# Probabilities times values in two halves of 256 queries, and the outputs' copies one step later, for the Fox and neighbourhood heads of a two-block fp32 transformer kernel

## The reference

```python
def one_block(i):
    ...
    sc = jnp.einsum('bhqd,bhkd->bhqk', qb, k).astype(jnp.float32) * scale
    sc = sc + (cb[..., :, None] - c[..., None, :])
    sc = jnp.where(pos[None, :] <= tq[:, None], sc, NEG_INF)
    p = jax.nn.softmax(sc, axis=-1)
    return jnp.einsum('bhqk,bhkd->bhqd', p.astype(v.dtype), v)
```

## Time and profile before

| | |
|---|---|
| median of 3 runs | 1406.56 us (1406.37 to 1409.49) |
| the profiled execution's own time | 1405.87 us |
| its span in the profile | 1403.9 us |
| PE busy | 1339.9 us (95%) |
| DVE busy | 690.7 us (49%) |
| ACT busy | 614.5 us (44%) |
| POOL busy | 663.2 us (47%) |
| DMA, mean | 91 GB/s |
| steps of the fox attention in which values are multiplied | from about 88 us to 169 us |
| the same of the na attention | from about 779 us to 881 us |

### The profile page before, as it was taken

How to read it: one execution, slowest core, us unless ns; L and a number is a source line. 1 busy time by engine, 2 the same in 40 slices (tenths; PEclk the granted TensorE clock), 3 DMA queues, 4 the chain that set the end, 5 groups by cost and what they waited for, 6 DMA issues and landing times.

```text
span 1403.9 us, 19167 instructions
## 1 busy us (share of the span) xinstructions
PE 1339.9 (95%) x6444; PEld 1110.3 (79%) x6444; DVE 690.7 (49%) x1247; ACT 614.5 (44%) x964; POOL 663.2 (47%) x884
## 2 busy tenths in 40 slices
PE   7899999789999999999999879999999999999997
PEld 5877887578888888888778668877778888888887
DVE  6477656672222222121588878757445555552111
ACT  5445555564434442343434454435345444442223
POOL 5432152255645555565464213555645545454550
PEclk9999999999999999999999999999999999999999
DMA  5322231222433332333472212323324333333331
GB/s 161 87 76 68 69 106 46 76 76 77 118 95 99 91 103 83 101 94 101 92 151 77 67 52 65 103 90 90 90 75 120 90 102 92 99 92 98 98 94 61
DMA packets 220326, 127.22 MB, mean 91 GB/s; under 512 B 8635, under 2 KB 215880, under 8 KB 220136
## 3 DMA queue, kind: packets, MB, share of 16 engines
q1 hardware_dynamic: 219751, 126.20, 32.1%
q10 hardware_dynamic: 513, 0.21, 0.1%
HBM read 117.56 MB, written 2.47 MB: 85 GB/s over the span
## 4 chain that ended last, share of the span: by engine, by line
PE 83%; DVE 8%; issue 4%; ACT 2%; DMA 1%; ACTq 0%; SPq 0%; POOL 0%; DVEq 0%; POOLq 0%
PE PS L749 27%; PE PS L751 26%; PE PS L750 26%; DVE PTL L1895 1%; PE PS L938 1%; DMA RAW<-in_w_out 1%; DVE NM L1860 1%; PE PS L914 0%; DVE SS L1619 0%; PE PS L915 0%; ACT PR L1318 0%; DVE KB L1709 0%; DMA ROWV<-in_diff_norm_g 0%; DVE PR L1854 0%; DVE XL L1623 0%
## 5 line engine op out<-in xcount | busy, mean ns | idle before, releaser
L721 POOL TENSOR_TENSOR WL<-RAW,WH 128x256 fp32r<-128x256 f32 x864 | 657.6, 792 | 709.2 <-ACT WH L1172 709.2
L749 PE MATMUL PS<-XH,WH 128*128 128x512 f32 x1072 | 423.4, 395 | 2.7 <-DVE X L1967 1.9
L1172 ACT ACTIVATE WH<-RAW 128x1024 fp32r<-128x1024 f32 (+1 forms) x220 | 229.1, 1043 | 443.1 <-PE PS L751 378.8
L751 PE MATMUL PS<-XH,WL 128*128 128x512 f32 x1072 | 418.3, 390 | 0.0
L750 PE MATMUL PS<-XL,WH 128*128 128x512 f32 x1072 | 418.1, 390 | 0.0
L749 PEld LDWEIGHTS PS<-XH,WH 128*128 128x128 f32 x1072 | 201.9, 188 | 44.2 <-DVE X L1967 2.6
L751 PEld LDWEIGHTS PS<-XH,WL 128*128 128x128 f32 x1072 | 201.5, 188 | 42.6
L750 PEld LDWEIGHTS PS<-XL,WH 128*128 128x128 f32 x1072 | 201.7, 188 | 39.6 <-issue 0.7
L749 PE MATMUL PS<-HH,WH 128*128 128x512 f32 (+1 forms) x374 | 141.0, 377 | 0.0
L751 PE MATMUL PS<-HH,WL 128*128 128x512 f32 (+1 forms) x374 | 140.8, 377 | 0.0
L750 PE MATMUL PS<-HL,WH 128*128 128x512 f32 (+1 forms) x374 | 140.8, 377 | 0.0
(11 more groups left out here) (326 smaller groups left out, 1851.5 us busy)
## 6 DMA issues: line engine op xcount, KB each, us to landing
RAW<-in_w_up SPq DMA_DIRECT2D x66, 512.0 KB, 3.8
RAW<-in_w_in SPq DMA_DIRECT2D x60, 512.0 KB, 3.9
RAW<-in_w_down SPq DMA_DIRECT2D x32, 512.0 KB, 3.7
RAW<-in_w_gate SPq DMA_DIRECT2D x22, 512.0 KB, 3.8
RAW<-in_w_out SPq DMA_DIRECT2D x16, 512.0 KB, 3.7
RAW<-in_w_down SPq DMA_DIRECT2D x16, 384.0 KB, 3.3
QB<-QA SPq DMA_DIRECT2D x24, 128.0 KB
KA<-KA SPq DMA_DIRECT2D x24, 128.0 KB
```

Source lines behind the costliest of these rows:

```text
L721: ins = pool.tensor_tensor(WL[:, s, cs], RAW[:, s % 2, cs], WH[:, s, cs].bitcast(F32), ALU.subtract)
L749: pe.matmul(out, ah, bh, start=start, stop=False)
L751: return pe.matmul(out, al, bh, start=False, stop=stop)
L1172: act.activation(WH[:, s, 0:width], RAW[:, s % 2, 0:width], ACT.Copy).then_inc(w_hi, 1)
```

## The change

For fox and na the product with the values is made in two halves. The first half, queries 0 to 255, stands in step 4 hd + 5, the second, queries 256 to 511, in step 4 hd + 7. Each half multiplies every key block that one of its two query blocks sees, at width 256: for fox 2 and 4 key blocks (6 and 12 matmuls), for na 3 and 3 (9 and 9 matmuls). A block of PTH and PTL that a half reads and no query block writes must be zero, hence two more `memset` of DVE before each of the two attentions. A new semaphore `pv_first` counts first halves: PTH's query blocks 0 and 1 of the next head wait for it, blocks 2 and 3 for `pv_ready` as before. ACT's copy of a head's result (MH, NAH) and DVE's subtraction (ML, NAL) move from step 4 hd + 7 to step 4 hd + 8. The diff heads do the same as before.

```diff
+            def pv_half(hd, half):
+                g = o0 + hd
+                pe.wait_ge(ptl_done, t0 + 4 * hd + 2 * half + 2)
+                if half == 0 and g >= 2:
+                    pe.wait_ge(o_free, g - 1)
+                vc = slice((hd // 2) * P, (hd // 2) * P + P)
+                q = slice(256 * half, 256 * half + 256)
+                kcs = [kc for kc in range(4) if any(keys_of(kind, qb)[0] <= kc < keys_of(kind, qb)[1]
+                                                    for qb in (2 * half, 2 * half + 1))]
+                for kc in kcs:
+                    ins = mm3(PS[:, OB + g % 2, q], mem["VH"][:, kc, vc], mem["VL"][:, kc, vc],
+                              mem["PTH"][:, kc, q], mem["PTL"][:, kc, q], kc == kcs[0], kc == kcs[-1])
+                ins.then_inc(pv_ready if half else pv_first, 1)
...
-                if i - 4 in ready_after and ready_after[i - 4] % 4 == 3:
-                    pv(ready_after[i - 4] // 4)
+                if i - 4 in ready_after and ready_after[i - 4] % 2 == 1:
+                    hd, qb = tr[ready_after[i - 4]]
+                    if kind != "diff":
+                        pv_half(hd, qb // 2)
+                    elif qb == 3:
+                        pv(hd)
...
-                    if o0 + hd > 0:
+                    if kind != "diff" and hd and qb < 2:
+                        act.wait_ge(pv_first, (8 if kind == "na" else 0) + hd)
+                    elif o0 + hd > 0:
                         act.wait_ge(pv_ready, o0 + hd)
...
+                if kind != "diff" and i - 5 in ready_after and ready_after[i - 5] % 4 == 3:
+                    hd = ready_after[i - 5] // 4
+                    act.wait_ge(pv_ready, o0 + hd + 1)
...
             step(dve.memset(M1[part][:, 3, 2 * P:3 * P].bitcast(F32), 0.0))
+            step(dve.memset(M1[part][:, 1, 0:P].bitcast(F32), 0.0))
...
+                if kind != "diff" and i - 5 in ready_after and ready_after[i - 5] % 4 == 3:
+                    hd = ready_after[i - 5] // 4
+                    bank = PS[:, OB + (o0 + hd) % 2, :]
+                    dve.wait_ge(oh_done, o0 + hd + 1)
...
             step(dve.memset(M2[part][:, 1, 3 * P:S].bitcast(F32), 0.0))
+            step(dve.memset(M2[part][:, 2, 0:P].bitcast(F32), 0.0))
```

More of the change, by code:

```diff
@@ L358, in program @@
     pv_ready = sem("pv_ready")
+    pv_first = sem("pv_first")
     oh_done = sem("oh_done")
@@ L943, in pv @@
                 pe.wait_ge(ptl_done, t0 + 4 * hd + 4)
-                if kind == "diff" and hd >= 2:
+                if hd >= 2:
                     pe.wait_ge(od_sum, hd - 1)
-                elif g >= 2:
+                else:
                     pe.wait_ge(o_free, g - 1)
-                vc = slice(hd * P, hd * P + P) if kind == "diff" else slice((hd // 2) * P, (hd // 2) * P + P)
-                for n, kc in enumerate((1, 0, 2, 3) if kind == "na" else range(4)):
+                vc = slice(hd * P, hd * P + P)
+                for n, kc in enumerate(range(4)):
                     qs = [qb for qb in range(4) if keys_of(kind, qb)[0] <= kc < keys_of(kind, qb)[1]]
@@ L1333, in attention @@
                 if i - 4 in ready_after and ready_after[i - 4] % 4 == 3:
-                    hd = ready_after[i - 4] // 4
                     if kind == "diff":
-                        norm_q = [hd]
-                    else:
[L1338 to L1345, removed]
+                        norm_q = [ready_after[i - 4] // 4]
+                if kind != "diff" and i - 5 in ready_after and ready_after[i - 5] % 4 == 3:
+                    hd = ready_after[i - 5] // 4
+                    act.wait_ge(pv_ready, o0 + hd + 1)
+                    r = slice((hd % 2) * HD, (hd % 2) * HD + HD)
+                    src = PS[r, OB + (o0 + hd) % 2, :]
+                    if kind == "fox":
+                        dst = MH[r, hd // 2, :]
+                    else:
+                        dst, src = grid3(NAH[r, hd // 2, :], "natural"), natural_of(src)
+                    act.activation(dst, src, ACT.Copy).then_inc(oh_done, 1)
                 if kind == "diff" and i == n + 2:
@@ L1899, in attention @@
                     hd = ready_after[i - 4] // 4
-                    bank = PS[:, OB + (o0 + hd) % 2, :]
                     if kind == "diff":
                         dve.wait_ge(pv_ready, o0 + hd + 1)
-                        dve.tensor_copy(ODR[:, hd, :], bank).then_inc(od_copy, 1)
+                        dve.tensor_copy(ODR[:, hd, :], PS[:, OB + (o0 + hd) % 2, :]).then_inc(od_copy, 1)
                         dve.wait_ge(od_copy, hd + 1)
@@ L1907, in attention @@
                         dve.tensor_tensor(SQ[:, 0, :], ODR[:, hd, :], ODR[:, hd, :], ALU.mult).then_inc(od_sq, 1)
-                    else:
[L1909 to L1917, removed]
+                if kind != "diff" and i - 5 in ready_after and ready_after[i - 5] % 4 == 3:
+                    hd = ready_after[i - 5] // 4
+                    bank = PS[:, OB + (o0 + hd) % 2, :]
+                    dve.wait_ge(oh_done, o0 + hd + 1)
+                    rr = slice((hd % 2) * HD, (hd % 2) * HD + HD)
+                    if kind == "fox":
+                        dve.tensor_tensor(ML[rr, hd // 2, :], bank[rr, :], MH[rr, hd // 2, :].bitcast(F32),
+                                          ALU.subtract).then_inc(o_free, 1)
+                    else:
+                        dve.tensor_tensor(grid3(NAL[rr, hd // 2, :], "natural"), natural_of(bank[rr, :]),
+                                          grid3(NAH[rr, hd // 2, :].bitcast(F32), "natural"),
+                                          ALU.subtract).then_inc(o_free, 1)
                 for it in fills_done(kind, i):
```

## The result

The changed kernel is faster: median 1399.99 us (1399.11 to 1400.34, 5 runs) against 1407.21 us (1406.37 to 1409.9, 5 runs), ratio 0.9943, 95% interval 0.9930 to 0.9956. That is 7 to 8 us, where 12.2 were forecast. In lines of the changed kernel 1 has to be added to the numbers of `mm3` (L750 to L752), the scores are L915, the transposes L939, the maximum L1882 (fox) or L1876 (na), PTH L1323, PTL L1917, the outputs L1366, L1935 and L1938.

What follows compares the result with a forecast made beforehand. PE was taken as the bound, with 19.9 us of waits for DVE's PTL the most to be had; na -9.0 and fox -3.2 gave -12.2 us, 1394.4 us by the median, range 1388.5 to 1403.

Steps and rivals of the forecast that it cites:

- The term for narrower products: PE's products in fox and na: width 256 costs 0.2 us more a head, 3.4 us for 16 heads.
- 11.45 was worked out: Na head periods, heads 0 to 3: 13.3 us become 11.45, 1.85 us less three times, -5.6 us.
- A: The forecast case for the whole kernel: 1390 to 1398 us, chance 0.62.
- rival B: Both attentions: head-row transfers and DVE keeping PE longer take gain back, leaving 6.5 us, 1400 us; chance 0.20.
- I take them all as gone: Fox: all of PE's stalls, below 1.4 us each, vanish, -6.3 us.
- The 1.5 us for transfers: Fox: head rows' transfers arrive late at three heads, 0.5 us each, +1.5 us.
- DVE waits some 0.6 us a head: Na periods: DVE waits 0.6 us a head for the next scores, making its period 11.2 us.
- the PTH of the next head's blocks 0 and 1 now waits for a half made two steps before: Both attentions: ACT's wait at PTH for the product should vanish, 20.1 + 26.7 us, with DVE's wait at PTL.
- Without that cover ... the head's path would still not grow by more than 0.2 us: First half ahead of block 3's transposes: uncovered 0.7 or 1.1 us a head, offset by the shorter second half.
- stall before head 0's product, 0.9 us, mostly filled: -0.7: Na's first product: PE's 0.9 us stall ahead of it mostly filled, -0.7 us.
- PE gets there about 1.1 us later relative to DVE, the stall falls to some 2.7 us, and the clock should hold: -1.6: Na head 4's product: stall falls from 3.76 to some 2.7 us, full clock held, -1.6 us.
- that exponential waits for the maximum behind the memsets: Na's beginning: two more memsets delay DVE's maximum and the exponential PE waits for, +0.5 us.

Runs made afterwards that it cites:

- narrow_only: Kernel before, product still whole and in place but made as 18 matmuls of width 256, with the change's four memsets: 1412.4 us, ratio 1.0024.
- step7_one_wait: Changed kernel with both halves in step 4 hd + 7 and without `pv_first`, PTH waiting for the whole product in all blocks: 1395.3 us, ratio 0.9907.
- outputs_late: Kernel before with only the output copies and subtractions one step later, product whole: 1402.4 us, ratio 0.9954.
- halves_step7: Changed kernel with both halves in step 4 hd + 7, one behind the other: 1392.8 us, ratio 0.9888.
- halves_step6: Changed kernel with the first half in step 4 hd + 6 instead of 4 hd + 5: 1396.2 us, ratio 0.9914.
- step7_outputs_old: Changed kernel with both halves in step 4 hd + 7 and the outputs back in their old step: 1394.2 us, ratio 0.9905.
- the two warm ones: 24 idle transposes at each of two PE stalls, added to the changed kernel (1396.6 us) and to halves_step7 (1392.6 us).

## Why the prediction was right and where it was not

**Right.** The sign and the range: PE's stalls in the two attentions shrank. The term for narrower products (3.4 us) was measured apart at 3.4 us. The na periods went from 13.3 to 11.74 us where 11.45 was worked out; -4.8 us for -5.6. DVE's waits at PTL and at the outputs came in at 2.6 and 4.0 us, with 4 named as the limit. PE's for PTL did not: 3.4 and 7.8 us, where under 2 and under 6 were named.

**The likeliest case did not come.** A was 1390 to 1398. The measured 1400.0 is the number of rival B, and of B's two parts only the smaller came: the 0.3 us by which a period is longer (11.74 for 11.45). The head rows' transfers never appear: no wait for KA, QA, KB or QB is in the two windows. That the total fits B is chance; the rest of the difference lies in the steps below. The 2.0 us a transfer that B's working cites from the Trainium skill stand, in the section named there, under the path of transfers issued by GpSimd; the ones here are issued by SP and ACT. No number of the sum used them.

**Fox came out by luck.** -2.8 us for -3.2, but not by its terms. "I take them all as gone" failed: 3.4 of the 6.3 us of PE's waits for PTL stayed. The 1.5 us for transfers never came. And apart from PE's idle time the fox stretch is 96.0 us, 95.9 before, where 1.6 us were added for the products; that these cost 1.6 us there shows in narrow_only alone, and what gave them back in the changed kernel was not separated. The errors cancel.

**The period's size.** The step "DVE waits some 0.6 us a head" was mis-sized: DVE is idle 0.9 us in 11.74. It was not the first half's place, as I thought after the result; the three periods are 34.8 to 35.5 us with the halves in step 5, 6 or 7, with one semaphore or two. What all these versions have in common is the way from the PTL through the second half and the next scores, or with one semaphore through PTH; that this way sets the 0.9 us is the likeliest reading, and no run tests it.

**The mechanism behind the gain.** The prediction put it on "the PTH of the next head's blocks 0 and 1 now waits for a half made two steps before". That step failed. The one semaphore of step7_one_wait leaves ACT's wait at 22.6 us in na and still keeps 13.1 of 15.8 us, and outputs_late gains 6.5 us with ACT's wait at PTH and DVE's at PTL no shorter. A wait's length told how long an engine stood, not what it held up. In fox the outputs' place was worth as much as the change (3.5 us in the traces, with whole products); in na it was mainly the length of the product behind the PTL, 2.03 us then, 1.18 after.

**The first half in step 4 hd + 5.** "Without that cover ... the head's path would still not grow by more than 0.2 us" and "stall before head 0's product, 0.9 us, mostly filled: -0.7" failed together: that stretch grew by 0.8 us, where -0.7 + 0.5 were forecast. The half delays block 3's transposes and the next scores, and DVE, which has no idle time to lose there, waits for these. In the changed kernel's DVE timeline, in na's step 6:

```profile
775.30 0.56 DVE L1876 CUSTOM_DVE_ANT_0 PR<-PS,BN 128x384 f32<-128x384 f32 x1 [0.45 <-PE PS L919]
```

Before, the maximum of this step began without a wait. The PTL that PE waits for begins 22.12 us after the first scores, where it was 20.46 (778.48 less 758.02) in the kernel before and is 20.7 with the first half in step 6 or 7. So 1.4 of the 1.7 us are the place, of which the wait shown is 0.45, and some 0.3 are left with the half in step 6 or 7 too, as in narrow_only with the memsets. The stall that the half should have filled is longer, not shorter:

```profile
779.60 0.41 DVE L1917 TENSOR_TENSOR PTL<-PS,PTH 128x256 fp32r<-128x256 f32 x1
```

```profile
780.07 0.39 PE L750 MATMUL PS<-PTH,VH 128*128 128x256 f32 x1 [1.46 <-DVE PTL L1917]
```

halves_step7 and halves_step6 measure the place: 1.4 us up to the end of na's first product and 3.0 us in fox.

**The clock.** "PE gets there about 1.1 us later relative to DVE, the stall falls to some 2.7 us, and the clock should hold: -1.6" failed. The first half of head 4 stands in step 21, and took the place of the 1.13 us that PE waited in step 22 before; in step 23 PE is then as far ahead of DVE as before, which still has the same work up to the PTL. The number was right for another placement: with both halves in step 7 the stall is 2.69 us and the clock holds. Behind the diff attention a fall that I had not looked for took 2.7 us in this trace.

**The memsets.** +0.5 us was forecast in na, at the wait of the earlier trace rows; that wait went from 0.92 to 0.96 us. The step "that exponential waits for the maximum behind the memsets" failed: ACT loads a function table at this place, and the exponential starts when that is done. In the kernel before the maximum was over at 762.26, and the load, which began at 761.48, at 762.76:

```profile
761.48 1.28 ACT L1318 ACT_TABLE_LOAD   x1
```

The memsets are paid further on, as DVE has no idle time up to block 3's PTL: some 0.3 us at the first product (narrow_only). ACT timeline of the changed kernel; DVE's maximum began at 761.82 and was over at 762.25:

```profile
760.95 1.28 ACT L1339 ACT_TABLE_LOAD   x1
762.28 0.51 ACT L1339 ACTIVATE PR<-PR,NM 128x256 f32<-128x256 f32 x1
```

**The account.** Forecast -12.2, trace -5.7. The difference of 6.5: fox 0.4, na's first product 1.0, periods 0.8, na's clock and head 4 together 2.1 (forecast -1.9 - 1.6, measured -3.0 and then +1.8 with head 5's 0.2 in it), heads 6 and 7 with the small stall 0.1 less, the stretch between with the clock behind the diff attention 2.2. By the medians, which are not bound to these two executions, 7.2 us were gained and 5.0 are missing.

## What to carry to other kernels

When a product waits for its last operand, put the part that does not need it close ahead of that wait, at best in the stall, and not two steps ahead, where it delays what the other engines wait for. Take a chain of waits as a list of suspects and undo them one at a time: taking 21 us of ACT's waits at PTH away was worth some 2.5 us, while moving the outputs, with 5.5 us of DVE's waits at ML, was worth as much in fox as the whole change. And look at the clock in more than one execution before a difference of 2 us in a stretch is put down to an edit. The version that beats both kernels is the changed one with both halves in step 4 hd + 7: 1392.8 us, 1.1% below the kernel before and 0.5% below the changed one.

## What the runs showed of the hardware that was not expected

The granted clock fell, or held, behind nearly equal stalls, and the length of the stall alone does not tell which. Behind 3.65 us it fell to 0.50 some 1.4 us after the stall's end in the changed kernel, and before the stall's end in halves_step6. Behind 3.01 us it held in the execution traced before and fell in the nine others with that stall. Behind 2.69 us it held in three (halves_step7, step7_one_wait, step7_outputs_old). Behind 2.37 us it held in the kernel before, behind 2.36 us it fell in narrow_only, and in outputs_late it fell at the end of one of 2.11 us. A fall cost some 1.4 to 2.7 us by the stretches above. The Trainium skill ("TensorE: Matmul & The Clock Gate", What's actually happening) calls the ramp variable from run to run of the same kernel. The traces agree, with low stretches at fox's beginning that end before 72 us in one execution and behind it in another. Some 2 us between two traces of these kernels can be that alone: the stretch between the attentions, in which the edits other than the two warm ones change next to nothing, ranges from 588.2 to 590.6 us.
